# Early expert tiles of the up stage: 512-column products, with the sums of their halves among VectorE's choice of experts

## The reference, cut to what matters

```
q = (xb @ w_q).reshape(128, 8, 2, 128)
s = einsum('thpk,pnk->thpn', q, sub_keys)          # 128 scores for each of two halves
s_top, i_top = top_k(s, 16)
cand = s_top[:, :, 0, :, None] + s_top[:, :, 1, None, :]
g_top, pos = top_k(cand, 16);  expert = cand_idx[pos];  g = softmax(g_top)
act = gelu(einsum('thkd,td->thk', peer_u[expert], xb))
y = einsum('thk,thkd->td', g * act, peer_v[expert])
```

## Time and profile before

| | us |
|---|---|
| median of 3 runs | 2539.65 |
| lowest, highest | 2537.67, 2540.99 |
| the profiled execution's own time | 2540.44 |
| its span, first to last instruction | 2538.6 |
| TensorE, VectorE busy | 2496.0, 2040.1 |
| ScalarE, GpSimd busy | 1487.1, 345.5 |
| mean granted TensorE clock | 0.996 |

### The profile page before, as it was taken

One profiled execution on the slowest core, in us unless ns is written; L12 is line 12 of the kernel. 1 busy time (PEld: TensorE's weight loads), 2 busy tenths in 40 slices (PEclk: granted clock), 3 DMA queues, 4 the chain that ended last, 5 costly groups with the idle time before them and its releaser, 6 DMA issues.

```text
span 2538.6 us, 44016 instructions
## 1 busy us (share of the span) xinstructions
PE 2496.0 (98%) x14932; PEld 2171.1 (86%) x14932; DVE 2040.1 (80%) x3770; ACT 1487.1 (59%) x2489; POOL 345.5 (14%) x212
## 2 busy tenths in 40 slices
PE   7999999999999999999999999999999999999998
PEld 6789988888888888889988888888888888889887
DVE  7789878899888887679888998666667886688766
ACT  4455576666655666655676666655654555463553
POOL 4017600000000004537400000000000001000000
PEclk8999999999999999999999999999999999999999
DMA  7854576776888884435667776555555455553654
GB/s 269 290 167 167 193 233 188 201 207 205 294 291 287 293 273 149 136 128 168 213 204 198 208 199 209 192 195 202 191 195 184 133 183 187 187 175 108 198 183 141
DMA packets 142991, 509.07 MB, mean 201 GB/s; under 512 B 19200, under 2 KB 19256, under 8 KB 142560
## 3 DMA queue, kind: packets, MB, share of 16 engines
q1 hardware_dynamic: 135600, 481.90, 57.0%
q0 software_dynamic: 7216, 24.85, 5.1%
HBM read 488.84 MB, written 1.07 MB: 193 GB/s over the span
## 4 chain that ended last, share of the span: by engine, by line
PE 90%; DVE 5%; ACT 2%; DMA 1%; issue 1%; POOL 1%; SPq 0%; DVEq 0%; ACTq 0%
PE ps L243 55%; PE ps L249 18%; PE ps L250 9%; PE ps L1528 2%; DMA weight_ring<-in_stream 1%; DVE weight_split L278 1%; POOL weight_split L278 1%; PE ps L2735 1%; PE ps L1492 1%; ACT weight_split L269 1%; DVE arena L745 0%; DVE hT_split L503 0%; PE ps L457 0%; DVE stat L628 0%; DVE x L625 0%
## 5 line engine op out<-in xcount | busy, mean ns | idle before, releaser
L269 ACT ACTIVATE weight_split<-weight_ring 128x1024 fp32r<-128x1024 f32 x800 | 848.4, 1062 | 251.4 <-DMA weight_ring<-in_stream 162.7
L243 PE MATMUL ps<-weight_split,hidden_split 128*128 128x512 f32 x3948 | 911.2, 390 | 0.0
L278 DVE TENSOR_TENSOR weight_split<-weight_ring,weight_split 128x1024 fp32r<-128x1024 f32 x653 | 791.7, 1221 | 145.3 <-ACT weight_split L269 141.4
L243 PEld LDWEIGHTS ps<-weight_split,hidden_split 128*128 128x128 f32 x3948 | 736.2, 188 | 156.0 <-issue 1.0
L249 PE MATMUL ps<-hT_split,weight_split 128*128 128x512 f32 x2000 | 722.9, 402 | 2.9 <-DVE arena L1787 1.5
L250 PE MATMUL ps<-hT_split,weight_split 128*128 128x256 f32 x2000 | 559.6, 280 | 0.0
L243 PE MATMUL ps<-hT_split,weight_split 128*128 128x256 f32 x3672 | 462.8, 285 | 2.7 <-DVE hT_split L503 0.8
L243 PEld LDWEIGHTS ps<-hT_split,weight_split 128*128 128x128 f32 x3672 | 447.2, 192 | 9.8 <-issue 6.0
L249 PEld LDWEIGHTS ps<-hT_split,weight_split 128*128 128x128 f32 x2000 | 375.9, 188 | 88.2 <-issue 3.0
L250 PEld LDWEIGHTS ps<-hT_split,weight_split 128*128 128x128 f32 x2000 | 377.8, 189 | 2.6
L278 POOL TENSOR_TENSOR weight_split<-weight_ring,weight_split 128x1024 fp32r<-128x1024 f32 x115 | 279.0, 2433 | 115.7 <-ACT weight_split L269 84.9
(11 more groups left out here) (381 smaller groups left out, 2077.1 us busy)
## 6 DMA issues: line engine op xcount, KB each, us to landing
weight_ring<-in_stream SPq DMA_DIRECT2D x912, 512.0 KB, 4.2
weight_split<-weight_ring POOLq DMA_DIRECT2D x32, 512.0 KB, 5.2
arena<-gate_rows SPq DMA_DIRECT2D x3, 512.0 KB, 4.4
x<-in_x SPq DMA_DIRECT2D x1, 1024.0 KB, 5.0
arena<-mlstm_m_rows POOLq DMA_DIRECT2D x1, 1024.0 KB, 6.5
arena<-in_ln_mix_g POOLq DMA_DIRECT2D x2, 512.0 KB, 5.3
arena<-in_ln_mix_b POOLq DMA_DIRECT2D x2, 512.0 KB, 7.1
arena<-in_ln_ffn_g POOLq DMA_DIRECT2D x2, 512.0 KB, 4.4
```

Source lines behind the costliest of these rows:

```text
L243: mm = pe.matmul(out_, stationary(s_part), moving(m_part), start=start and n == 0, stop=stop and n == 2, skip_group_check=True)
L269: act.activation(wsplit[:, n % SPLITS, HIGH, :], ring[:, slot(POS[n]), :], ACT.Copy).then_inc(high_ready, 1)
L278: eng.tensor_tensor(w[:, REST, :], ring[:, slot(POS[n]), :], w[:, HIGH, :].bitcast(fp32), ALU.subtract).then_inc(split_ready, 1)
```

## The change

WIDE begins at tile 4 instead of 30, in both layers. The sums of tiles 4 to 31 are put into VectorE's choice of experts: one after each of the 8 heads, five among the small instructions, three in each run of 16 selections, one after each half of a reduction (which is cut in two for it), and five after the choice; those of 32 and 33 follow the first two rests that VectorE makes. HEAD is 34: GpSimd makes the rests of 34 up tiles in each layer, and the part of the stream in which row tiles are mixed in, `places_turned` and the copies after it come six tiles later. The exponentials come after tile 17. `summed` itself is moved, not changed.

```
--- before.py
+++ after.py
@@ -48,9 +48,9 @@
 
 SEGMENTS = [("ada", "a", 16), ("mlstm", "s", 8), ("mlstm_v", "sa", 8), ("mlstm_o", "saa", 7), ("mlstm_o_end", "sa", 1),
             ("mlstm_out", "s", 4), ("mlstm_out_ada", "sa", 1), ("mlstm_out_end", "s", 3),
-            ("peer0q", "s", 16), ("up0", "s", 28), ("up0_ada", "ssa", 8), ("up0_end", "s", 12), ("up0_late", "s", 72), ("down0", "ssa", 56), ("down0_end", "s", 8), ("down0_late", "s", 8),
+            ("peer0q", "s", 16), ("up0", "s", 34), ("up0_ada", "ssa", 8), ("up0_end", "s", 6), ("up0_late", "s", 72), ("down0", "ssa", 56), ("down0_end", "s", 8), ("down0_late", "s", 8),
             ("sb", "s", 8), ("sb_q", "s", 8), ("sb_v", "s", 8), ("sb_out", "s", 8),
-            ("peer1q", "s", 16), ("up1", "s", 28), ("up1_ada", "ssa", 8), ("up1_end", "s", 12), ("up1_late", "s", 72), ("down1", "s", 64), ("down1_end", "s", 64),
+            ("peer1q", "s", 16), ("up1", "s", 34), ("up1_ada", "ssa", 8), ("up1_end", "s", 6), ("up1_late", "s", 72), ("down1", "s", 64), ("down1_end", "s", 64),
             ("hy", "s", 32), ("mlp0", "s", 64), ("gla", "s", 32), ("mlp1", "s", 64)]
 FIRST = {}
 POS, ADA_POS, KINDS, BOUNDS = [], [], [], []
@@ -74,14 +74,14 @@
 OUT_GROUPS = [4 if n == 3 else GROUPS for n in range(9)]
 SRC_PARTS = {0: 3, 1: 5, 2: 5, 4: 5}
 GATE_ROW = (2, 5, 10, 13)
-HEAD, BODY = 28, 24
+HEAD, BODY = 34, 24
 
 STEP_AT = [j for j in range(52, 125) if (j - 52) % 8 != 7]
 STEPS_BY = [sum(at <= j for at in STEP_AT) for j in range(128)]
 FIRST_STEP = STEP_AT[0]
 EARLY = 51
-EXP_AT = 14
-WIDE = [j for j in range(128) if 30 <= j < 126 and j != 51]
+EXP_AT = 17
+WIDE = [j for j in range(128) if 4 <= j < 126 and j != 51]
 
 
 def slot(pos):
@@ -1701,6 +1701,15 @@
                 both(lambda tb: dve.max_index(idx(tb)[:, 8:16], val(tb)[:, 8:16], spare(tb)))
 
 
+            def summed(j):
+
+                dve.wait_ge(halves_copied, wide_count(l, j))
+                first = first_of(4 + j % 3)
+                if j >= FIRST_STEP:
+                    dve.tensor_tensor(first, second_halves, first, ALU.add).then_inc(halves_summed, 1)
+                else:
+                    dve.tensor_tensor(acts(j), acts(j), first, ALU.add).then_inc(halves_summed, 1)
+
             for s in range(16):
                 dve.wait_ge(pr_s_out, 16 * l + s + 1)
                 top16(lambda tb: pr_s[:, s % 2, tb], lambda tb: pr_s2[:, tb], lambda tb: pr_val[:, tb, s], lambda tb: pr_idx[:, tb, s])
@@ -1716,6 +1725,7 @@
             after_dve(last)
             for h in range(8):
                 top16(lambda tb: pr_cand[:, tb, h], lambda tb: pr_c2[:, tb], lambda tb: pr_g[:, tb, h], lambda tb: pr_pos[:, tb, h])
+                summed(4 + h)
 
             g = pr_g.rearrange("p a h k -> p (a h) k")
             e = pr_e.rearrange("p a h k -> p (a h) k")
@@ -1724,18 +1734,23 @@
 
             flat = pr_pos.rearrange("p a h k -> p (a h k)")
             m1, m2, place = pr_block[:, 0], pr_block[:, 1], pr_block[:, 2]
+            summed(12)
             after_dve(dve.tensor_copy(place, flat))
             after_dve(dve.tensor_scalar(m1, place, float(BLOCKS[1][3]), None, ALU.is_ge), dve.tensor_scalar(m2, place, float(BLOCKS[2][3]), None, ALU.is_ge))
             after_dve(dve.tensor_tensor(pr_mix[:, 0], m1, m2, ALU.add),
                       dve.scalar_tensor_tensor(out=pr_mix[:, 1], in0=m1, scalar=2.0, in1=m2, op0=ALU.mult, op1=ALU.add))
+            summed(13)
             after_dve(dve.tensor_scalar(pr_shift, pr_mix[:, 0], -1.0, 4.0, ALU.mult, ALU.add),
                       dve.tensor_scalar(pr_mask, pr_mix[:, 1], -4.0, 15.0, ALU.mult, ALU.add))
+            summed(14)
             after_dve(dve.tensor_tensor(pr_half[:, 0], flat, pr_shift, ALU.logical_shift_right),
                       dve.tensor_tensor(pr_half[:, 1], flat, pr_mask, ALU.bitwise_and))
+            summed(15)
             after_dve(dve.tensor_copy(pr_halff, pr_half.rearrange("p n (a c) -> p n a c", a=2)))
             first = pr_halff[:, 0].rearrange("p a c -> p (a c)")
             after_dve(dve.scalar_tensor_tensor(out=first, in0=m1, scalar=-2.0, in1=first, op0=ALU.mult, op1=ALU.add))
             after_dve(dve.scalar_tensor_tensor(out=first, in0=m2, scalar=-6.0, in1=first, op0=ALU.mult, op1=ALU.add))
+            summed(16)
 
             for n in range(2):
                 idx = pr_idxf.rearrange("p t (h a) k -> p t h a k", a=2)[:, :, :, n, :]
@@ -1743,12 +1758,19 @@
                 for a in range(16):
                     last = dve.scalar_tensor_tensor(out=pr_eq[:, n, :, a].rearrange("p (t h k) -> p t h k", t=TB, h=8), in0=at, scalar=float(a),
                                                     in1=idx[:, :, :, a].unsqueeze(3).broadcast_to([128, TB, 8, 16]), op0=ALU.is_equal, op1=ALU.mult)
+                    if a in (3, 8, 13):
+                        summed(17 + 5 * n + a // 5)
                 after_dve(last)
-                after_dve(dve.tensor_reduce(pr_sel[:, n].rearrange("p a c -> p (a c)"), pr_eq[:, n], AX.X, ALU.add))
+                for tb in range(TB):
+                    last = dve.tensor_reduce(pr_sel[:, n, tb], pr_eq[:, n, tb * 128:(tb + 1) * 128], AX.X, ALU.add)
+                    summed(20 + 5 * n + tb)
+                after_dve(last)
             dve.wait_ge(pr_exp, l + 1)
             after_dve(dve.tensor_reduce(pr_sum[:, 0], e, AX.X, ALU.add))
             after_dve(dve.reciprocal(pr_sum[:, 1], pr_sum[:, 0]))
             dve.tensor_tensor(g, e, pr_sum[:, 1].unsqueeze(2).broadcast_to([128, 16, 16]), ALU.mult).then_inc(pr_chosen, 1)
+            for j in range(27, HEAD - 2):
+                summed(j)
 
             def up_rest(j):
                 if added(j):
@@ -1760,15 +1782,6 @@
                 if HEAD <= j < HEAD + 16 and (j - HEAD) % 2:
                     ada_dve((104 if l else 40) + (j - HEAD) // 2, edge_b)
 
-            def summed(j):
-
-                dve.wait_ge(halves_copied, wide_count(l, j))
-                first = first_of(4 + j % 3)
-                if j >= FIRST_STEP:
-                    dve.tensor_tensor(first, second_halves, first, ALU.add).then_inc(halves_summed, 1)
-                else:
-                    dve.tensor_tensor(acts(j), acts(j), first, ALU.add).then_inc(halves_summed, 1)
-
             def weigh(q):
 
                 g, tokens = step_weights(q), slice(STEP * q, STEP * q + STEP)
@@ -1824,7 +1837,9 @@
 
             splits_until(dve, tu + HEAD)
             up_rest(HEAD)
+            summed(HEAD - 2)
             up_rest(HEAD + 1)
+            summed(HEAD - 1)
             for j in range(HEAD, 129):
                 if j + 1 in STEP_AT:
                     if with_step(j + 1) == 0:
```

## The result

The changed kernel takes 2561.72 us (2561.38 to 2562.76, 4 runs), the kernel before 2538.78 us beside it: ratio 1.0089, 95% interval [1.0077, 1.0101], so 22.9 us or 0.9% slower. The forecast was 2566.7, between 2552 and 2575.

What follows compares the result with a forecast made beforehand. TensorE's tiles were taken to bound the kernel, with VectorE's choice setting the pace after the change. Choice's end 303.5 + 13.1 + 7.8 = 324.4, plus 5.3, makes tile 31 13.5 us late; two layers 27 us: 2566.7 on the median, range 2552 to 2575.

Steps and rivals of the forecast that it cites:

- The last link: From choice's end to tile 31: sum of tile 27, activation, copy, high part, GpSimd's rest; 5.3 us.
- The gain of the wide form: 26 early up tiles at 0.05 us, 1.3 us a layer; with tile 18's 0.4 us hold, 1.7, if TensorE is never held.
- The first wait: TensorE ahead of tile 7 waits 3.1 us, as tile 4's sum comes only after VectorE's first head.
- The heads: Next seven heads: 3.24 us each with its sum against 2.83 a wide tile; TensorE loses 2.9 us more.
- 23 sums at 0.57: Sums of tiles 4 to 26 ahead of the choice's end on VectorE add 13.1 us.
- the rule on the port: VectorE instructions on SBUF alone wait out GpSimd's 2.40 us rests, sums reading PSUM do not; 7.8 us more waiting in the choice.
- Rival B: The port rule is too narrow, some sums also wait for a rest: five × 2.4 us a layer, 2591; chance 0.03.
- The mis-sized term: One of L1733 and L1734, in VectorE's choice, meets two GpSimd rests back to back: 4.7 us, called the frailest term.
- my 13.5: Tile 31 starts 13.5 us late in each layer, including the first waits and all of the gain.
- Rival C: TensorE's clock falls to 0.50 after tile 7's wait; some 3 us left in each layer, 2573; chance 0.04.
- Rival A: After the last head, waits shrink because GpSimd, starved by late sums, leaves VectorE alone: 2549 to 2556, say 2553; chance 0.15.
- Rival D: Not slower: without L1713's waits VectorE reaches sum 4 before 245.3, deciding at 3 us saved; 2536; chance 0.03.

Runs made afterwards that it cites:

- e1: Changed kernel with tiles 4 to 11 narrow again, so the eight sums among the heads are gone; 2542.86 us, ratio 1.0015 to the kernel before.
- e5: Changed kernel with the sums of tiles 4 to 11 one place earlier each, the first ahead of the first head; 2557.23 us against 2542.0, ratio 1.0056.
- e6: Changed kernel with an unawaited stand-in addition behind each of the eight sums among the heads; 2570.93 us against 2542.0 for the kernel before, ratio 1.011.
- e7: Changed kernel with operands of the choice moved to PSUM, nothing left out; 2542.54 us against 2542.0 for the kernel before, ratio 1.0001.
- e9: The kernel of e7 with tiles 17, 18 and 19 narrow; 2537.28 us against 2539.22 for the kernel before, ratio 0.9991.
- e3: Changed kernel with tiles 4 to 33 narrow and an unawaited stand-in addition on VectorE at each sum's place; 2539.20 us, ratio 1.0002 to the kernel before.
- e2: Changed kernel with tiles 4 to 26 narrow and without their sums, all else of the change kept; 2538.49 us, ratio 0.9997 to the kernel before.
- e4: Changed kernel with GpSimd filling the 34 early up tiles' rests with zeros instead of reading and subtracting; 2535.24 us, ratio 0.9981 to the kernel before.

## Why the prediction was right, step by step

**One relation carries it.** The delay was worked out from the end of the choice, followed by a sum, an activation, a copy, a high part and a rest up to tile 31. If that holds, tile 31 is late by the shift of the choice's end less a constant, in every kernel in which the sums are awaited:

| kernel | choice ends later by, us | less 7.8 | tile 31 late by, layer 0 |
|---|---|---|---|
| changed kernel | 18.2 | 10.4 | 10.4 |
| e1 | 9.5 | 1.7 | 1.7 |
| e5 | 15.0 | 7.2 | 7.2 |
| e6 | 22.0 | 14.2 | 14.2 |
| e7 | 7.6 | −0.2 | −0.2 |
| e9 | 6.1 | −1.7 | −0.8 (held by rests) |
| e3, sums not awaited | 14.4 | 6.6 | −0.5 |

The constant is measured in the first row; e1 was run before it was written down, e5, e6 and e7 after it. In layer 1 the relation holds within 0.15 us. e2 and e4 aren't in the table, since nothing holds TensorE in them: the choice ends 5.7 and 5.5 us later and tile 31 is 0.8 and 2.3 us early; that 5.5 less 7.8 gives e4's −2.3 is chance. The constant contains the 0.65 of the transposes, which my sum had counted off: on its footing it is 7.1, and I had put it at 7.4. The last row shows that it is a wait and no load.

**The last link was not the one I named.** In the changed kernel the chain behind the choice's end gets to the end of tile 31's rest at 328.11, but TensorE comes to tile 31 only at 328.4. It was last held at tile 29, which started at 322.71 behind a rest that ended at 322.57; ScalarE could make that tile's high part after the sum of tile 25, done at 317.92, 4.9 us ahead of the end of the choice. What VectorE does between that sum and the end is the same in the five kernels whose figures fit, so the table can't tell the two; the last 1.1 us of waiting, at L1771, need not have cost TensorE anything.

**The gain of the wide form.** Forecast 0.05 us a tile. In e4, where nothing holds TensorE, tile 45 is 1.7 us early in layer 1, just the 1.3 + 0.4; in layer 0 it is 2.2, as the tiles from 39 on took 2.77 us there. So the gain is real, but no kernel that leaves nothing out got near it.

**The first wait.** Forecast: sum at 248.4, hold of 3.1 us. Measured 248.34 and 3.05.

**The heads.** Forecast 3.24 us a sum, measured 3.24 to 3.25, in both layers.

**23 sums at 0.57 and the rule on the port.** The sums last 0.65 to 0.69 beside rests, with 0.57 to the next instruction, and none waited inside. For the additions e4 and e7 show that it is GpSimd's reads against VectorE's second SBUF operand: without the reads, or with one operand in PSUM, they last 2.1 us instead of 8.7. Rival B is out. For instructions with two SBUF operands this is the rule of the Trainium skill ("SBUF — State Buffer", "Who interferes with whom"), and the traces agree from both sides. My own wording, that an instruction on SBUF alone waits out a rest, was both too wide and taken from two kinds of rows: the MAX8 of the heads work on SBUF alone and take 0.42 us for two in the earlier trace rows and 0.42 in e4, with rests and without, while the casts and the instructions on one tensor and constants (TENSOR_SCALAR: L1739, in e1 L1746) read one SBUF tensor and do wait, in e4 even for a fill that reads nothing. What makes those wait wasn't tested by itself; with their input in PSUM (e7, L1740) they didn't.

**The mis-sized term.** It is the 4.7 us that the prediction has for L1733 or L1734. In the order of its list of waits the runs show (new line numbers): L1732 1.3, L1739 4.3 for the two, sum 14 1.0, L1747 2.2 where I had 4.7, sum 18 0.75, L1771 1.1, and 0.4 at sum 19 that I had not. The others were right within 0.2. I had it wait for two rests on end; the rests at 283.94 did stand on end (4.99 us for two), but L1747 was done at 286.64, after the first. An instruction of VectorE that was already waiting got in between two rests. So the choice ended 18.2 later and not 20.9. On the footing of my 13.5, with the transposes counted off, a layer lost 11.1 and 11.0 us: 2.7 less by the choice's end, 0.3 more by the constant. Two layers make 22.1, against the 27 forecast and the 22.9 of the medians. That the 22.1 comes so near the medians is partly luck: by tile 50 the steps of 2.77 have brought the two layers down to 20.6, and 1.8 us of the spans' difference is traced to nothing.

**The first wait is no term of the sum**, as I had said of the 3.1 and 2.9 us: in e5 TensorE starts tile 7 with most of its hold gone, and the relation stands. It would decide only where the choice's end does not.

**Rival C, the clock.** I had named a fall of the clock behind tile 7 as a sign that I was wrong. It fell, in layer 0 and in layer 1 (0.54 in the 3 us behind the hold there), and it cost nothing here: tile 7's products were done by 255.6, and ScalarE, itself held by the sums, came for them only at 257.33. e6 shows the same within one execution: the clock fell in layer 0 and not in layer 1, and tile 31 is 14.2 and 14.3 us late. In e5 there was no fall either, and the relation between the choice's end and tile 31 was the same. The sign was ill chosen; the price I gave it, 3 us a layer, was too high.

**Rival A**, that the waits shrink for a starved GpSimd: half true. GpSimd stood idle 6.03 us once, yet its rests came in pairs afterwards, and L1739 met both of one pair.

**Rival D** named the right place: with the additions at 2.1 us the sum of tile 4 comes 6.4 us sooner, tile 7 is not held, and the loss is gone. Both e4 and e7 freed the later waits too, and both are far beyond the 3 us at which I had put the point, so the point itself isn't tested. D's gain of 3.4 us shows in e4 alone.

What stays open: how much of the 1.7 us a layer, of which e9 has 0.2 at tile 30, a different order on ScalarE, high part ahead of the activation by one more tile, would give back. It wasn't tried.

## What to carry to other kernels

Before an awaited step is put into another engine's list, write down when that engine will come to it, and follow the list to its end: the delay is set by the last awaited steps near the list's end, and neither the first wait nor the number of steps tells it. Look in that list for rows that last several times what their size costs elsewhere (here 2.63 against 0.47 us); they are waits in disguise, they move when anything before them moves, and they may be cheap to remove by giving one operand another memory. And weigh the gain per step (0.05 us) against the price per step on the other engine (0.57 us): it pays only while that engine has room.

## What the hardware showed that I had not expected

- An instruction of VectorE waiting for GpSimd's rest was let in before GpSimd's next one, which followed on its heels: L1747 ended 2.62 us after it began, under two rests that together took 4.99. But two such instructions in a row (L1739) each waited out one rest, 4.78 us.
- After a stand of TensorE of 3.05 us the granted clock fell to 0.50, and it stayed there until 254.35. With the shorter holds of e5 (at most 1.7 us in layer 0's stretch) it stayed at 1.00. But the length of a stand doesn't tell it alone: of two equal ones in e6, 3.18 and 3.19 us, the first was followed by a fall and the second was not.
- Not every instruction on SBUF waits for GpSimd: MAX8 took 0.42 us for two with GpSimd's rests and without, while one TENSOR_SCALAR with a single SBUF operand waited out a rest (2.49 us, e1) and another a mere fill (1.28 us for two instead of 0.49, e4).
- Some 5 us of VectorE work can be worth 4 or 9 us, by the rests that it happens to meet: e1 took 4.6 us of sums off and gained 8.7 a layer, e6 put 5.0 on and lost 3.8.
